# One 128-column operand for the high and low values in a softmax attention branch, and one instruction for two heads

## The reference

```python
s = jnp.einsum('bghqd,bgkd->bghqk', qb, kwb)
p_win = masked_softmax(s, mw)
o_win = jnp.einsum('bghqk,bgkd->bghqd', p_win, vwb.astype(jnp.float32))
...
o = g[..., 0:1] * to_bshd(o_cmp) + g[..., 1:2] * to_bshd(o_slc) + g[..., 2:3] * to_bshd(o_win)
```

## Time and profile before

| | us |
|---|---|
| median of 3 runs | 1579.07 |
| lowest and highest | 1578.88, 1581.48 |
| the profiled execution | 1579.92 |
| its span, first to last instruction | 1578.2 |
| PE busy | 1488.9 |
| DVE busy | 837.6 |
| ACT busy | 686.4 |
| POOL busy | 205.5 |
| mean granted TensorE clock | 0.982 |

### The profile page before, as it was taken

The page is one execution under the profiler, slowest core; times in us unless marked ns, Lnnn a source line. Parts: engine busy times, 40 slices in busy tenths (PEclk is TensorE's granted clock), DMA queues, the critical chain, the costliest instruction groups (busy, mean ns, idle before and its releaser), DMA issues.

```text
span 1578.2 us, 22125 instructions
## 1 busy us (share of the span) xinstructions
PE 1488.9 (94%) x8593; PEld 1252.4 (79%) x8593; DVE 837.6 (53%) x1444; ACT 686.4 (43%) x1305; POOL 205.5 (13%) x309
## 2 busy tenths in 40 slices
PE   4999998999989999999989998988999999999997
PEld 2788866678988888888888886668988888888986
DVE  5767645577464444432275345875654444422364
ACT  4555535377443222322353235886542232222453
POOL 0000000144310000000130003653300000000211
PEclk9999999799999999999999999999999999999999
DMA  9533340002213333333403331003033333333321
GB/s 375 211 94 101 120 153 9 1 2 68 94 55 102 96 93 95 102 96 93 147 1 107 95 92 54 5 24 108 1 94 93 96 103 93 93 111 97 114 81 54
DMA packets 40531, 143.06 MB, mean 91 GB/s; under 512 B 4464, under 2 KB 6528, under 8 KB 39808
## 3 DMA queue, kind: packets, MB, share of 16 engines
q1 hardware_dynamic: 38240, 129.55, 25.8%
q0 software_dynamic: 1632, 11.52, 2.0%
q10 hardware_dynamic: 576, 0.85, 0.2%
HBM read 139.81 MB, written 2.10 MB: 90 GB/s over the span
## 4 chain that ended last, share of the span: by engine, by line
PE 81%; DVE 8%; ACT 5%; issue 3%; POOL 1%; DMA 1%; DVEq 0%; SPq 0%; POOLq 0%; ACTq 0%
PE B L277 24%; PE B L278 23%; PE B L279 23%; PE B L1646 3%; ACT T L560 2%; PE B L1730 1%; PE B L1528 1%; PE B L1866 1%; POOL T L480 1%; PE B L1625 1%; DVE WADA L1069 1%; DMA X<-in_x 1%; DVE WL L1023 1%; DVE KEPT_L L1021 1%; DVE X L1034 1%
## 5 line engine op out<-in xcount | busy, mean ns | idle before, releaser
L277 PE MATMUL B<-UH,WH 128*128 128x512 f32 (+1 forms) x1120 | 420.7, 376 | 17.1 <-DVE UL L1078 6.3
L278 PE MATMUL B<-UL,WH 128*128 128x512 f32 (+1 forms) x1120 | 417.0, 372 | 0.0
L279 PE MATMUL B<-UH,WL 128*128 128x512 f32 (+1 forms) x1120 | 416.9, 372 | 0.0
L277 PEld LDWEIGHTS B<-UH,WH 128*128 128x128 f32 x1120 | 212.1, 189 | 57.7 <-DVE UL L1041 7.6
L560 ACT ACTIVATE WH<-RAW 128x1024 fp32r<-128x1024 f32 x178 | 186.6, 1051 | 137.2 <-DMA RAW<-in_stream 117.0
L278 PEld LDWEIGHTS B<-UL,WH 128*128 128x128 f32 x1120 | 212.3, 190 | 36.3
L279 PEld LDWEIGHTS B<-UH,WL 128*128 128x128 f32 x1120 | 212.2, 189 | 36.4
L1023 DVE TENSOR_TENSOR WL<-RAW,WH 128x1024 fp32r<-128x1024 f32 x98 | 121.9, 1246 | 165.6 <-ACT WH L560 165.4
L560 ACT ACTIVATE T<-B 128x256 f32<-128x256 f32 (+3 forms) x207 | 96.0, 466 | 126.1 <-PE B L279 64.5
L1323 DVE TENSOR_TENSOR WL<-RAW,WH 128x1024 fp32r<-128x1024 f32 x80 | 98.1, 1226 | 76.7 <-ACT WH L560 74.0
L560 ACT ACTIVATE T<-T 128x512 f32<-128x512 f32 (+3 forms) x131 | 68.6, 525 | 134.2 <-DVE T L1327 119.2
(11 more groups left out here) (340 smaller groups left out, 2928.9 us busy)
## 6 DMA issues: line engine op xcount, KB each, us to landing
RAW<-in_stream SPq DMA_DIRECT2D x202, 512.0 KB, 3.6
WADA<-in_w_ada SPq DMA_DIRECT2D x4, 2048.0 KB, 18.8
RAW<-in_stream SPq DMA_DIRECT2D x16, 384.0 KB, 3.2
WADA<-in_w_ada SPq DMA_DIRECT2D x4, 1024.0 KB, 18.4
W<-in_w POOLq DMA_DIRECT2D x2, 2048.0 KB, 11.3
X<-in_x SPq DMA_DIRECT2D x2, 1024.0 KB, 10.5
DECAY<-in_decay POOLq DMA_DIRECT2D x1, 2048.0 KB, 8.1
X<-in_x POOLq DMA_DIRECT2D x2, 1024.0 KB, 8.4
```

Of the source, the lines that this page charges most:

```text
L277: nc.tensor.matmul(out, lh, rh, start=start, stop=False, **kw)
L278: nc.tensor.matmul(out, lh, rl, start=False, stop=False, **kw)
L279: return nc.tensor.matmul(out, ll, rh, start=False, stop=stop, **kw)
```

## The change

In the NSA branch the high and the low values of a head now lie beside each other in one tile, `VN`, so that [high, low] is one fixed operand of 128 columns. Two matmuls for each block (with the low and with the high part of the weights) take the place of three, and write all 128 partitions of the bank: high values in the first 64, low values in the last 64. The two halves have to be added: behind ACT's copy of the first half, `at_x`, DVE adds the second half to it (`at_sum`, eight adds of 64 x 512), and what waited for `at_x` now waits for `at_sum`. With it the product low x low is also added, which was left out before. `BD` has 128 columns, of which the last 64 are zero.

PSUM is allocated as four tensors of two banks, so that one instruction can reach over the banks of both heads. In both branches the high part (ACT), the low part and the reciprocals (DVE) of a pair are now one instruction each, and in NSA also the maxima. Their events count up by two and their waits ask for both heads.

```diff
--- before.py
+++ after.py
@@ -101,7 +101,7 @@
         DECAY = hb("DECAY", 48, [P, NH, SEQ])
         QNH, QNL = hb("QNH", 64, [P, 4, SEQ], F32R), hb("QNL", 72, [P, 4, SEQ], F32R)
         KNH, KNL = hb("KNH", 80, [P, 2, SEQ], F32R), hb("KNL", 84, [P, 2, SEQ], F32R)
-        VNH, VNL = hb("VNH", 88, [P, 4, 256], F32R), hb("VNL", 92, [P, 4, 256], F32R)
+        VN = hb("VN", 88, [P, 4, 4, 2, HD], F32R)
         Y_H = hb("Y_H", 48, [P, KT, SEQ])
         MRH, MRL = hb("MRH", 0, [P, 4, SEQ], F32R), hb("MRL", 8, [P, 4, SEQ], F32R)
         GR = hb("GR", 16, [P, 4, SEQ])
@@ -111,8 +111,8 @@
         W2K = hb("W2K", 52, [P, 2, 2, P])
         W2V = hb("W2V", 54, [P, 2, HD])
         HV4 = hb("HV4", 55, [P, 2, 2, 4, 32])
-        BD = hb("BD", 57, [P, 2, 4, HD])
-        KCF = hb("KCF", 59, [P, 4, 32])
+        BD = hb("BD", 57, [P, 2, 4, P])
+        KCF = hb("KCF", 61, [P, 4, 32])
 
         KPH, KPL = hb("KPH", 48, [P, 4, P], F32R), hb("KPL", 50, [P, 4, P], F32R)
         SCT = at("SCT", OFF_U + 4 * KB, [P, 2, SEQ])
@@ -195,7 +195,8 @@
         VEC2 = small("VEC2", [P, 32])
         V2_F2PRE, V2_F2POST, V2_PLE, V2_SB, V2_BAND = 0, 8, 16, 24, 28
 
-        B = [nc.alloc_psum_tensor(f"B{n}", [P, SEQ], F32) for n in range(8)]
+        TWO = [nc.alloc_psum_tensor(f"TWO{n}", [P, 2, SEQ], F32) for n in range(4)]
+        B = [TWO[n // 2][:, n % 2, :] for n in range(8)]
 
         def sem(name):
             return ctx.enter_context(nc.semaphore(name))
@@ -226,9 +227,9 @@
             def __init__(self, name, goes_on=None, base=0):
                 self.sem, self.n, self.base = (goes_on.sem if goes_on else sem(name)), 0, base
 
-            def mark(self, ins):
-                self.n += 1
-                ins.then_inc(self.sem, 1)
+            def mark(self, ins, by=1):
+                self.n += by
+                ins.then_inc(self.sem, by)
                 return ins
 
         def wait(eng, s, value):
@@ -291,7 +292,7 @@
             "pt_hi pt_lo pp ep pl_s".split())}
 
 
-        pl_y, at_x, at_m, at_hi, at_lo = (Event(n) for n in "pl_y at_x at_m at_hi at_lo".split())
+        pl_y, at_x, at_sum, at_m, at_hi, at_lo = (Event(n) for n in "pl_y at_x at_sum at_m at_hi at_lo".split())
         f_g, f_s, f_u, f_h, f_hh, f_hl = (sem(n) for n in "f_g f_s f_u f_h f_hh f_hl".split())
         NSA = {n: Event("nsa_" + n) for n in "s max exp rec sc tr hi lo pv".split()}
         BAND = {n: Event("", NSA[n], 64) for n in "s max exp rec sc tr hi lo pv".split()}
@@ -302,6 +303,7 @@
         T_RING = [T[10], T[11], T[0], T[1]]
         R_BANK = [B[3], B[4], B[5], B[6]]
         S_BANK, PT_BANK = [B[2], B[3], B[4], B[5]], [B[6], B[7]]
+        S_PAIR, PT_PAIR = TWO[1:3], TWO[3]
         Z_RING, SP_RING, P_RING = ([T[n] for n in ring] for ring in ((0, 1, 8, 9), (2, 3, 6, 7), (4, 5, 10, 11)))
 
         Q_RING = [T[8], T[9], T[6], T[7]]
@@ -357,11 +359,10 @@
         def nsa_unit(h, kind, i):
             g, j, L = h // 4, h % 4, (i + 1) * P
             rows, cols = slice(64 * g, 64 * g + 64), slice(i * P, (i + 1) * P)
-            o = slice(kind * P + g * HD, kind * P + (g + 1) * HD)
             return {"h": h, "i": i, "L": L, "q": (QNH[rows, j, cols], QNL[rows, j, cols]),
                     "k": (KNH[rows, kind, 0:L], KNL[rows, kind, 0:L]), "mask": MASKB[:, 0, :], "bias": None,
                     "gate": GLS[:, i, 3 * h + kind + 1:3 * h + kind + 2],
-                    "v": lambda b: (VNH[:, b, o], VNL[:, b, o])}
+                    "both": lambda b: VN[:, b, 2 * kind + g, :, :]}
 
         def band_unit(h, i):
             L = (i + 1) * P
@@ -684,7 +685,7 @@
                             E["v_hi"].mark(f(VRH[:, t, :], B[4 + t][:, :], ACT.Copy))
                         else:
                             f(GLS[:, t, :], B[4 + t][:, 256:280], ACT.Sigmoid)
-                            E["v_hi"].mark(f(VNH[:, t, :], B[4 + t][:, 0:256], ACT.Copy))
+                            E["v_hi"].mark(f(VN[:, t, :, 0, :], B[4 + t][:, 0:256].rearrange("p (c e) -> p c e", c=4), ACT.Copy))
 
 
             for m in range(25):
@@ -737,12 +738,11 @@
                 for m in range(N + 6):
                     ahead(m)
                     if 3 <= m < N + 3:
-                        for s in range(2):
-                            u = 2 * (m - 3) + s
-                            i = units[u]["i"]
-                            wait(act, tag["tr"], u + 1)
-                            wait(act, tag["pv"], u - 3)
-                            tag["hi"].mark(f(AH2[:, u % 4, 0:(i + 1) * P], PT_BANK[s][:, 0:(i + 1) * P], ACT.Copy))
+                        u, at = 2 * (m - 3), slice(2 * (m - 3) % 4, 2 * (m - 3) % 4 + 2)
+                        L = units[u]["L"]
+                        wait(act, tag["tr"], u + 2)
+                        wait(act, tag["pv"], u - 2)
+                        tag["hi"].mark(f(AH2[:, at, 0:L], PT_PAIR[:, :, 0:L], ACT.Copy), 2)
                     if m < N:
                         for s in range(2):
                             u = 2 * m + s
@@ -1151,7 +1151,7 @@
                         if d < 16:
                             E["v_lo"].mark(tt(VRL[:, t, :], B[4 + t][:, :], VRH[:, t, :], ALU.subtract))
                         else:
-                            E["v_lo"].mark(tt(VNL[:, t, :], B[4 + t][:, 0:256], VNH[:, t, :], ALU.subtract))
+                            E["v_lo"].mark(tt(VN[:, t, :, 1, :], B[4 + t][:, 0:256].rearrange("p (c e) -> p c e", c=4), VN[:, t, :, 0, :], ALU.subtract))
 
             def compressed_keys_values():
 
@@ -1171,7 +1171,7 @@
                 for g in range(2):
                     for j in range(4):
                         rows = slice(32 * j, 32 * j + 32)
-                        E["cmp_bd"].mark(v.tensor_copy(BD[rows, g, j, :], B[6][rows, P + HD * g:P + HD * (g + 1)]))
+                        E["cmp_bd"].mark(v.tensor_copy(BD[rows, g, j, 0:HD], B[6][rows, P + HD * g:P + HD * (g + 1)]))
 
 
             dve.wait_ge(decay_here, 16)
@@ -1204,7 +1204,7 @@
                     v.memset(BD[:, :, :, :], 0.0)
                     chain.done(v.memset(HV4[:, :, :, :, :], 0.0))
                     for KP in (KPH, KPL):
-                        chain.done(v.tensor_copy(KP[:, :, :], BD[:, :, :, :].rearrange("p g j e -> p (g j e)").rearrange("p (j c) -> p j c", j=4)))
+                        chain.done(v.tensor_copy(KP[:, :, :], BD[:, 0, :, :]))
                     for hf in range(2):
                         src = HIDT[:, 1, hf, :].rearrange("p (g n) -> p g n", g=2).unsqueeze(2).broadcast_to([P, 2, 4, NC])
                         E["cmp_dup"].mark(v.tensor_copy(HV4[:, hf, :, :, 0:NC], src))
@@ -1239,37 +1239,42 @@
                 N = len(units) // 2
                 for m in range(N + 6):
                     ahead(m)
-                    if m < N:
+                    if m < N and units[2 * m]["bias"] is None:
+                        u = 2 * m
+                        wait(dve, tag["s"], u + 2)
+                        tag["max"].mark(v.tensor_reduce(NMAX[:, u % 8:u % 8 + 2], S_PAIR[m % 2][:, :, 0:units[u]["L"]], AX.X,
+                                                        ALU.max, negate=True), 2)
+                    elif m < N:
                         for s in range(2):
                             u = 2 * m + s
                             L, top, S = units[u]["L"], NMAX[:, u % 8:u % 8 + 1], S_BANK[u % 4]
                             wait(dve, tag["s"], u + 1)
-                            if units[u]["bias"] is None:
-                                ins = v.tensor_reduce(top, S[:, 0:L], AX.X, ALU.max, negate=True)
-                            else:
-                                wait(dve, tag["tr"], u - 7)
-                                dve.wait_ge(bias_here if units[u]["h"] < 4 else bias_rest, 16)
-                                ins = v.tensor_tensor_reduce(S_RING[u % 8][:, 0:L], S[:, 0:L], units[u]["bias"], -1.0, 3.0e38,
-                                                             ALU.add, ALU.min, top)
+                            wait(dve, tag["tr"], u - 7)
+                            dve.wait_ge(bias_here if units[u]["h"] < 4 else bias_rest, 16)
+                            ins = v.tensor_tensor_reduce(S_RING[u % 8][:, 0:L], S[:, 0:L], units[u]["bias"], -1.0, 3.0e38,
+                                                         ALU.add, ALU.min, top)
                             tag["max"].mark(ins)
                     if 3 <= m < N + 3:
-                        for s in range(2):
-                            u = 2 * (m - 3) + s
-                            i = units[u]["i"]
-                            wait(dve, tag["hi"], u + 1)
-                            tag["lo"].mark(tt(AL2[:, u % 4, 0:(i + 1) * P], PT_BANK[s][:, 0:(i + 1) * P],
-                                              AH2[:, u % 4, 0:(i + 1) * P], ALU.subtract))
+                        u, at = 2 * (m - 3), slice(2 * (m - 3) % 4, 2 * (m - 3) % 4 + 2)
+                        L = units[u]["L"]
```

(30 more changed lines are left out.)

## The result

The changed kernel takes 1616.34 us (median of four runs, 1604.4 to 1634.1), against 1580.28 for the kernel before: a ratio of 1.0198, with a 95% interval of 1.0111 to 1.0286. The ratio is that of the runs that count as fast, without the one of 1634.1 us, which counts as slow and is the one profiled. It is slower, as forecast, but by about 36 us by the medians (31 by the ratio) where 19.6 were summed up, and outside the range. Its runs differ far more than those of before, and that is the result's main content: two of the four took 1604.4 and 1605.2 us with a mean granted TensorE clock of 0.975, the others 1627.5 and 1634.1 us with 0.958 and 0.950. In a second series all five runs of the same kernel took 1613.1 to 1614.2 us (0.965 to 0.969).

The account below looks back on a forecast made before the run. TensorE, busy 94% of the span, was taken as the bound in NSA, and a loop through three engines in the banded branch. Terms summed to 19.6 us over 1579.9, given as 1599 us; forecast 1593 to 1603, eight-in-ten range 1585 to 1605.

Parts of the forecast that it names:

- The value products: NSA products: 320 matmuls at 0.11 us, 35.2 us, in place of 480 at 0.06, 28.8 us: 6.4 us more.
- the rival of 0.06 us: NSA products: 128-column float32r load hides under 0.06 us of moving columns, giving 9.6 us; chance 0.15 in all.
- The four-block pairs: NSA, second four-block pair: transposes stall 1.2 us for the merged subtraction, not 0.3; 0.9 us more, four times, 3.6 us.
- The three-block pairs: NSA: merged copy and subtraction end 0.05 to 0.15 us behind PE; eight times about 0.1, 0.8 us.
- The turn: NSA, one head to the next: PE stalls 1.1 us for later exponentials and adds, at three turns, 3.3 us.
- p2: Output projection after NSA: its weight chunk on DVE waits behind two adds of 1.3 us, partly covered; 1.0 us more.
- The banded branch: Second block: merged copies and subtractions wait for both heads; 3 us more, bounds 2 us less to 6 us more.
- the end of the branch: NSA's last four pairs, without scores to hide behind: merged durations cost 1.5 us beyond the longer products.
- The clock: NSA rounds: granted TensorE clock taken to stay at 1.00, its full 2.4 GHz; no term in the sum.
- Rival (3): NSA: stalls let PE's clock fall, one more slow stretch adding 3 to 6 us, 1602 to 1606 us; chance 0.12.

Follow-up runs that it names:

- wide_only: Changed kernel with the 128-column operand and adds, but copies, subtractions, reciprocals and maxima for each head as before: 1586.67 us against 1580.15, ratio 1.0040.
- fill_again: Changed kernel plus four 128x512 matmuls before the scores in each NSA step whose transposes wait for the four-block pair, run again: 1604.01 us.
- copy_sub: Kernel before with only the copies and subtractions merged over both heads: 1595.68 us, ratio 1.0093.
- after_again: Changed kernel unaltered, run again in a second series: five runs of 1613.06 to 1614.22 us, ratio 1.0200.
- max_rec: Kernel before with only the NSA maxima and the reciprocals merged over both heads: 1582.9 us, ratio 1.0007.
- pairs_only: Kernel before with merged copies, subtractions, reciprocals and maxima; products still three matmuls with 64 columns: 1595.01 us, ratio 1.0096.
- split_four: Changed kernel with copy and subtraction for each head again for four-block pairs alone, in both branches: 1598.05 us, ratio 1.0105.
- merge_four: wide_only with copy and subtraction merged for the four-block pairs alone, in both branches: 1593.12 us, ratio 1.0073.
- fill_beside: Changed kernel plus four 128x512 matmuls one step earlier than in fill_again, where TensorE does not wait: 1605.44, 1606.45, 1614.41 and 1626.31 us.

## Why the prediction was wrong, step by step

**The value products.** Right in the mechanism: 0.11 us for 128 float32r columns, the upper bound that I took. Of the 6.4 us some 5.8 are seen: in `wide_only` the products of a four-block pair take 1.91 us to the next scores in place of 1.62, so 1.45 for the 40 blocks of a round. With 0.4 us saved on the compressed matmuls and 0.25 of waiting for the adds its second round is 1.3 us longer: 5.2 in four rounds. The Trainium skill's figure of about 81 ns for 128 moving columns ("TensorE: Matmul & The Clock Gate", "Back-to-back issue gap") is between the two rates of this case, 60 and 111 ns, and holds for neither. By the Trainium skill's rule on fast weight load ("TensorE: Matmul & The Clock Gate", "Weight-path perf modes") the rival of 0.06 us would have come true; for float32r the traces show that rate with 64 columns and not with 128.

**The four-block pairs.** Right: PE's wait of 1.24 us was forecast as 1.2. Net it is 1.1 us each for 0.9: the transposes start 1.54 us after the mask where 0.12 is usual, and then take 0.31 less, because the second head is no longer held.

**The three-block pairs.** The term of 0.8 us was too small. The transposes behind them start 0.44 us after the mask in the changed kernel and not 0.12: eight times 0.3, 2.5 us. I had the merged copy begin 0.1 us after the last transpose and ended 0.1 behind PE; with a margin that thin the handovers between engines, some 0.1 us each, decide, and I rounded them away.

**The turn.** PE reaches the compressed matmul 1.60 us after the first transpose where it was 0.97: 0.6 us and not 1.1. But in the third round the adds and the gate products hold the low parts behind them, which I had ruled out: 1.2 us (26.0 against 24.8). Three turns cost 3.1 us, near the 3.3 by another way. In p2 the wait for the weight chunk is 1.7 us in `wide_only` for 0.6 before, my 1.0; but in the changed kernel's traces and in `fill_again` there is no such wait at all, so there the term is 0.6 less and not 1.0 more. The last round takes 21.3 us in `fill_again` for 17.0; without the four- and three-block pairs (1.1 and 0.6) and 0.5 for what `wide_only` adds there, 2.2 us or so are left for my 1.5. The banded branch costs 4.3 us where I took 3.0, inside its bounds, and it is in `copy_sub` too (4.4), so from the pair's copy and subtraction as said.

**The sum without the clock** was 19.6 us; the fastest runs have 22.7 to 24.9 over before. They took 1603.1 to 1605.2 us: above the forecast of 1593 to 1603, and at the upper end of the range, one just over it. In the two stages themselves the sum was near: `fill_again`, the nearest trace at full clock, has 16.2 us more than before between its first compressed matmul and p2 and 4.4 in the banded branch. Of its other 4 us 3.5 lie in front of that matmul, where the slow stretches differ from trace to trace (`after_again` is 0.5 us ahead of before there). That it came so near is in part luck: the four- and three-block pairs, the end of the branch and the banded branch cost 0.8, 1.7, 0.7 and 1.3 us more than said, the products (net, in `wide_only`) and p2 1.2 and 1.6 less.

**The clock** is the step that failed. The sum forecast the 1.2 us waits and priced each at 0.9 us; it has no term for the clock, and takes the 0.11 us of a product at 1.00 throughout. Rival (3) had the mechanism as far as the runs show it: stalls let PE's clock fall. It had 0.12 of chance and "3 to 6 us", for one stretch like that of the last banded rows. A stretch here lasts some 24 us, costs 8.6, and comes up to three times and once in part: 9 to 30 us over the runs at 1604 in 9 of the changed kernel's 13. Why it falls in some rounds and runs and not in others stays open. That 1602 to 1606 has the fastest runs in it is luck: in them that fall is not seen, and the other terms made the time. The upper end of the range, 1605, left out what the rival could bring more than once: each round has the same wait, so what can happen in one can happen in four. And at half clock a whole stretch counts, not only its product loads. A rival that acts per round has to be priced per round.

## What to carry to other kernels

Merging two instructions into one saves overhead on an engine, which was worth nothing here, where that engine is not the bound (`max_rec`); between a producer and a consumer that wait for each other it takes away the overlap of the two, and here it cost 14.9 us for 176 instructions less (`pairs_only`). Count the width of a fixed operand, and not only the moving columns: with 128 of these a float32r operand of 128 columns took 0.11 us where one of 64 took 0.06, so two for three was a loss. And where TensorE is the bound, a wait that a change adds, of 1.2 us here, can put its clock at risk, once for each time the wait recurs; what helped was to shorten the wait (`split_four`), or to put matmuls without use into that very wait, where they cost nothing.

## What the runs showed that I had not expected

No single one of the parts was enough for the long fall. Two kernels with the same wait of 1.2 us and the same products differ in it (`merge_four`: 0 of 5 runs; the changed kernel: 9 of 13), and with the same 0.9 us of extra matmuls the long fall came in 0 of 8 runs with them in the wait and in 2 of 4 with them one step before it. In a slow stretch PE is busy without a gap, 24.00 of 24 us, before the clock comes back to 1.00. In the traces of the changed kernel the long wait that followed one of 24 us, 8 to 9 us on, was then the start of the next stretch in all five cases; in `fill_beside`, 9 us on, it was not so in either of two cases.

The compressed matmul with 128 columns in place of 64 was no dearer, and why stays open. From its start to what follows the one block of products behind it, `wide_only` takes 1.13 us where it was 1.32, with the same 512 moving columns and a wider, dearer block.
